# Two-block transformer kernel (RWKV-7, differential attention, gated recurrence) on one core: the down projection of each gated feed-forward moved into its gate/up loop

## The reference, cut to what matters

```python
def swiglu_ffn(h, w_gu, w_down):
    gate, up = jnp.split(h @ w_gu, 2, axis=-1)
    return (jax.nn.silu(gate) * up) @ w_down
# third block: depthwise 3x3 convolution on the gate branch
gc = lax.conv_general_dilated(g2, taps, (1, 1), 'SAME', ..., feature_group_count=f) + conv_b
return (a * jax.nn.gelu(gc, approximate=False)) @ w_down
...
x = x + swiglu_ffn(rms_norm(x, g_ffn[layer]), ffn_w_gu[layer], ffn_w_down[layer])
```

## Time and profile before

| | us |
|---|---|
| median of 3 runs (1563.83 to 1584.23) | 1569.13 |
| profiled execution, span | 1571.6 |
| PE busy in it | 1331.9 (85%) |
| DVE busy | 999.0 (64%) |
| ACT busy | 663.0 (42%) |
| POOL busy | 294.2 (19%) |
| mean granted TensorE clock | 0.913 |

### The profile page before, as it was taken

The page is one execution under the profiler, slowest core; times in us unless marked ns, Lnnn a source line. Parts: engine busy times, 40 slices in busy tenths (PEclk is TensorE's granted clock), DMA queues, the critical chain, the costliest instruction groups (busy, mean ns, idle before and its releaser), DMA issues.

```text
span 1571.6 us, 23032 instructions
## 1 busy us (share of the span) xinstructions
PE 1331.9 (85%) x9712; PEld 1238.5 (79%) x9712; DVE 999.0 (64%) x1265; ACT 663.0 (42%) x844; POOL 294.2 (19%) x229
## 2 busy tenths in 40 slices
PE   3997899997788998989876888999788957887887
PEld 3876889886778997978554778999787947877887
DVE  4859644544489996563755354444549964899953
ACT  3644312114332343456336446543354544544433
POOL 0000332431034551000000001110006502244300
PEclk7978999999888998989987889999898978999999
DMA  7413100000366995544331234545451303444342
GB/s 260 137 67 109 53 1 1 1 1 1 110 238 219 319 323 187 186 135 160 111 104 54 84 118 156 164 163 186 150 182 61 126 8 108 155 141 134 120 148 83
DMA packets 124534, 198.91 MB, mean 127 GB/s; under 512 B 3472, under 2 KB 111376, under 8 KB 118544
## 3 DMA queue, kind: packets, MB, share of 16 engines
q1 hardware_dynamic: 119680, 167.19, 32.5%
q0 software_dynamic: 3456, 25.17, 4.5%
q10 hardware_dynamic: 1296, 5.09, 0.9%
HBM read 196.38 MB, written 1.05 MB: 126 GB/s over the span
## 4 chain that ended last, share of the span: by engine, by line
PE 50%; DVE 26%; issue 10%; ACT 7%; POOL 4%; DMA 2%; DVEq 0%; ACTq 0%; POOLq 0%; SPq 0%
PE bank L564 11%; PE bank L565 11%; PE bank L566 11%; DVE work L1736 6%; DVE ring_r L1479 5%; PE bank L730 3%; PE bank L742 3%; ACT high L1005 2%; PE bank L750 2%; POOL part L1402 2%; POOL ring_r L1409 2%; PE bank L622 1%; DMA buf<-in_wide 1%; DVE buf L1961 1%; DVE buf L1950 1%
## 5 line engine op out<-in xcount | busy, mean ns | idle before, releaser
L564 PE MATMUL bank<-part,high 128*128 128x256 f32 (+1 forms) x2224 | 644.6, 290 | 108.1 <-DVE part L1487 67.9
L565 PE MATMUL bank<-part,high 128*128 128x256 f32 (+1 forms) x2224 | 636.4, 286 | 0.0
L566 PE MATMUL bank<-part,ring_r 128*128 128x256 f32 (+1 forms) x2224 | 635.8, 286 | 0.0
L1479 DVE TENSOR_TENSOR ring_r<-ring,high 128x2048 fp32r<-128x2048 f32 (+2 forms) x172 | 337.4, 1964 | 317.6 <-ACT high L1005 316.9
L564 PEld LDWEIGHTS bank<-part,high 128*128 128x128 f32 (+1 forms) x2224 | 431.5, 194 | 120.1 <-issue 95.4
L565 PEld LDWEIGHTS bank<-part,high 128*128 128x128 f32 (+1 forms) x2224 | 432.3, 194 | 1.1 <-issue 1.0
L566 PEld LDWEIGHTS bank<-part,ring_r 128*128 128x128 f32 (+1 forms) x2224 | 431.1, 194 | 0.1
L1005 ACT ACTIVATE high<-ring 128x2048 fp32r<-128x2048 f32 (+1 forms) x172 | 300.9, 1752 | 171.4 <-PE bank L566 162.5
L1402 POOL TENSOR_TENSOR part<-buf,part 128x256 fp32r<-128x256 f32 x66 | 80.5, 1220 | 536.6 <-ACT part L1059 536.5
L1397 POOL TENSOR_TENSOR work<-buf,con 128x512 f32<-128x512 f32 x56 | 71.1, 1284 | 289.3 <-DVE buf L1660 229.2
L2055 DVE SCALAR_TENSOR_TENSOR buf<-buf,col 128x256 f32<-128x256 f32 x176 | 110.9, 630 | 5.5
(11 more groups left out here) (264 smaller groups left out, 1606.6 us busy)
## 6 DMA issues: line engine op xcount, KB each, us to landing
ring<-in_wide SPq DMA_DIRECT2D x122, 1024.0 KB, 5.7
ring<-in_down SPq DMA_DIRECT2D x48, 704.0 KB, 4.1
buf<-in_wide POOLq DMA_DIRECT2D x24, 1024.0 KB, 5.9
buf<-in_wide ACTq DMA_DIRECT2D x2, 1024.0 KB, 6.5
con<-in_cons SPq DMA_DIRECT2D x1, 1664.0 KB, 11.4
ring<-in_wide SPq DMA_DIRECT2D x2, 576.0 KB, 7.1
buf<-in_ctx_t ACTq DMA_DIRECT2D x1, 1024.0 KB, 4.8
out_t<-resid SPq DMA_DIRECT2D x8, 128.0 KB, 2.1
```

What stands on the lines that cost most here:

```text
L564: mm(bank, ah, bh, start=start, stop=False)
L565: mm(bank, ah, bl, start=False, stop=False)
L566: return mm(bank, al, bh, start=False, stop=stop)
L1479: v.tensor_tensor(low, raw, hi.bitcast(F32), ALU.subtract).then_inc(sem("unit_low"), 1)
```

## The change

The down units are laid out by pair of f instead of by output block: unit c is 128x2048, two f by 1024 output columns, 11 units instead of 16. Unit c-2 follows the two gate/up units of pair c in the stream, and `down_pair(c - 2)` follows `gate_up(c)` on TensorE (`LAG` 2): 48 matmuls that add two f to all eight output blocks, which stay open in banks 0 to 3, two to a bank. Gate/up and side jobs go round over banks 4 to 7. VectorE's multiply frees a gate/up bank instead of GpSimd. The products live in 8 slots, reused once the down unit that read them was used. The last two pairs run after the loop, block by block (96 matmuls). GpSimd's rest of a unit is tied to unit numbers, so that with a down unit in between it looks ahead two f, not three. The splits of the units behind the last down units move behind the next norm's root on ScalarE and behind the applied norm on VectorE (`down_ahead`).

```diff
+PAIR_N = FT // 2
+LAG = 2
+ACTS = 8
+FFN_BANKS = (4, 5, 6, 7)
...
+    def ffn(n):
+        for c in range(PAIR_N):
+            out.extend((f"gu{n}", c, half, "wide", W_AT[f"gu{n}"][0] + c) for half in range(2))
+            if c >= LAG:
+                out.append((f"dn{n}", c - LAG, 0, "down", PAIR_N * n + c - LAG))
+        out.extend((f"dn{n}", c, 0, "down", PAIR_N * n + c) for c in range(PAIR_N - LAG, PAIR_N))
...
     if stage[:2] == "dn":
-        return FT // 2, P
+        return 2, D
...
+        def plan_ffn(n, after_gate=lambda c: (), after_first=()):
+            for c in range(PAIR_N):
+                for i in range(2):
+                    place(("gu", n, 2 * c + i), FFN_BANKS)
+                    unit_job(f"gu{n}", c, i, ("gu", n, 2 * c + i))
+                for key in after_gate(c):
+                    place(key, FFN_BANKS)
+                if c == LAG:
+                    for j in range(KT // 2):
+                        place_at(("dn", n, j), j)
+                if c >= LAG:
+                    unit_mid(f"dn{n}", c - LAG, 0)
+            for key in after_first:
+                place(key, FFN_BANKS)
+            for c in range(PAIR_N - LAG, PAIR_N):
+                unit_job(f"dn{n}", c, 0, ("dn", n, KT // 2 - 1))
...
         def act_value(f):
-            return buf[2 + f // 8][:, f % 8, :]
+            return buf[2][:, f % ACTS, :]
...
+        def wait_act_slot(eng, n, f):
+
+            if f >= ACTS:
+                wait_unit(eng, UNIT_NO[(f"dn{n}", (f - ACTS) // 2, 0)])
...
+                def down_tile(n, f, cb, w):
+
+                    bank = banks[jobs[("dn", n, cb // 2)][0]][:, cb % 2 * S:(cb % 2 + 1) * S]
+                    wl, wh = (z[:, f % 2, cb * P:(cb + 1) * P] for z in w)
+                    mm(bank, wh, act_high(f), start=f == 0 and cb % 2 == 0, stop=False, skip_group_check=True)
+                    mm(bank, wh, act_low(f), start=False, stop=False, skip_group_check=True)
+                    return mm(bank, wl, act_high(f), start=False, stop=f == FT - 1, skip_group_check=True)
+
+                def down_pair(n, c):
+                    w = arrived(f"dn{n}", c, 0)
+                    if c == 0:
+                        for j in range(KT // 2):
+                            open_bank(("dn", n, j))
+                    for f in (2 * c, 2 * c + 1):
+                        pe.wait_ge(sem("act_ready"), FT * n + f + 1)
+                        for cb in range(KT):
+                            last = down_tile(n, f, cb, w)
+                    last.then_inc(sem("unit_used"), 1)
+
+                def feed_forward(n, after_gate=lambda c: None, after_first=lambda: None):
+                    for c in range(PAIR_N):
+                        gate_up(n, c)
+                        after_gate(c)
+                        if c >= LAG:
+                            down_pair(n, c - LAG)
+                    w = [arrived(f"dn{n}", c, 0) for c in range(PAIR_N - LAG, PAIR_N)]
                     for cb in range(KT):
                         if cb == 1:
                             after_first()
...
+                        for f in range(FT - 2 * LAG, FT):
+                            if cb == 0:
+                                pe.wait_ge(sem("act_ready"), FT * n + f + 1)
+                            last = down_tile(n, f, cb, w[f // 2 - PAIR_N + LAG])
+                        if cb % 2:
+                            close(last, ("dn", n, cb // 2))
...
                 def gate_high(n, f):
-                    eng.wait_ge(sem("act_raw"), FT * n + f + 1)
+                    wait_freed(eng, ("gu", n, f))
+                    wait_act_slot(eng, n, f)
...
                         if f % 2:
                             between(f // 2)
+                            if f // 2 >= LAG:
+                                ahead(f"dn{n}", f // 2 - LAG, 0)
 
                 def down(n, norm_no):
 
-                    for cb in range(KT + 2):
...
+                    for j in range(KT // 2):
+                        wait_freed(eng, ("dn", n, j))
+                        square(norm_no, resid, j)
                     root(norm_no)
+                    for c in range(PAIR_N - LAG, PAIR_N):
+                        ahead(f"dn{n}", c, 0)
...
                 def act_low_part(n, f):
...
-                    pool.sem_inc(free[jobs[key][0]], 1)
...
+                def rests_to(stage, u):
+
+                    while rests[0] < FT and UNIT_NO[(stage, rests[0] // 2, rests[0] % 2)] - HIGHS <= u:
+                        low_rest(stage, rests[0])
+                        rests[0] += 1
...
                 for f in range(FT):
-                    if f + HIGHS < FT:
-                        low_rest("gu2", f + HIGHS)
+                    rests_to("gu2", UNIT_NO[("gu2", f // 2, f % 2)])
                     act_low_part(2, f)
...
-                        key = ("dn", n, cb)
-                        for half in range(2):
-                            ahead(f"dn{n}", cb, half)
+                        key = ("dn", n, cb // 2)
                         wait_full(eng, key)
-                        release(add(cb, bank_of(key)[:, 0:S]), key)
...
+                        ins = add(cb, bank_of(key)[:, cb % 2 * S:(cb % 2 + 1) * S])
+                        release(ins, key) if cb % 2 else own.go(ins)
...
-                    v.tensor_tensor(act_value(f), gate_tmp(f), bank_of(key)[:, cols], ALU.mult).then_inc(sem("act_raw"), 1)
+                    wait_act_slot(eng, n, f)
+                    release(v.tensor_tensor(act_value(f), gate_tmp(f), bank_of(key)[:, cols], ALU.mult), key)
...
-                    if f % 2 and f >= 5:
+                    if f % 2 == 0 and f >= 4:
                         modulation_out(f // 2 - 2)
...
                 norm_apply(resid, "hkv", lambda kt: pcol("kv_g", kt))
+                down_ahead(0)
                 norm_apply(resid, "hq", lambda kt: pcol("g_mix1", kt))
...
 def down_chunks(w):
-    w = np.asarray(w).reshape(FT, P, KT, P)
-    return w.transpose(2, 1, 0, 3).reshape(KT, P, FT * P)
+    w = np.asarray(w).reshape(PAIR_N, 2, P, D)
+    return w.transpose(0, 2, 1, 3).reshape(PAIR_N, P, 2 * D)
```

More of the change, by code:

```diff
@@ L74, in wide @@
         out.extend((stage, i, half, "wide", W_AT[name or stage][0] + first + i) for i in range(n) for half in range(2))
-    def down(n):
-        out.extend((f"dn{n}", i, half, "down", KT * n + i) for i in range(KT) for half in range(2))
-    for stage, n in (("k", 2), ("lora1", 1), ("r", 2), ("v", 2), ("o", 2), ("gu0", 11)):
+    def ffn(n):
[4 more added lines that the diff above has]
+        out.extend((f"dn{n}", c, 0, "down", PAIR_N * n + c) for c in range(PAIR_N - LAG, PAIR_N))
+    for stage, n in (("k", 2), ("lora1", 1), ("r", 2), ("v", 2), ("o", 2)):
         wide(stage, n)
-    down(0)
+    ffn(0)
     wide("ak", 2, "kv")
@@ L170, in build, with place_at, place @@
         uses = [0] * NBANK
-        order = []
-        def place(key):
-            b = len(order) % NBANK
+        turn = {}
+        def place_at(key, b):
             jobs[key] = (b, uses[b])
             uses[b] += 1
-            order.append(key)
+        def place(key, among=tuple(range(NBANK))):
+            turn[among] = turn.get(among, -1) + 1
+            place_at(key, among[turn[among] % len(among)])
         unit_end = {}
@@ L257, in build @@
         place(("norm", 1))
[L258 to L262, removed]
+        plan_ffn(0, lambda c: [("ada", c - 1)] if c >= 1 else (), (("ada", 10), ("ada", 11), ("norm", 2)))
         place(("norm", 3))
@@ L289, in build @@
         place(("norm", 4))
[L290 to L299, removed]
+        plan_ffn(1, lambda c: [("csum", d, t) for d in range(2) for t in range(TT)] if c == 4 else
+                 [("cstate", d) for d in range(2)] if c == 7 else ())
         place(("norm", 5))
@@ L328, in build @@
         place(("norm", 6))
-        for c in range(11):
-            plan_gu(2, c)
-        plan_down(2)
+        plan_ffn(2)
         place(("norm", 7))
@@ L635, in down_proj @@
                             after_first()
-                        bank = open_bank(("dn", n, cb))
-                        for half in range(2):
[L638 to L646, removed]
-                                last.then_inc(sem("unit_used"), 1)
+                        for f in range(FT - 2 * LAG, FT):
[4 more added lines that the diff above has]
+                            close(last, ("dn", n, cb // 2))
                 pe.wait_ge(sem("con_in"), 16)
@@ L814, in ada_sum @@
                     close(last, ("ada", c))
-                for c in range(11):
-                    gate_up(0, c)
-                    if c >= 1:
-                        ada_sum(c - 1)
                 def rest_of_context():
@@ L879, in _, with context_states @@
                 norm(4)
-                for c in range(11):
-                    gate_up(1, c)
+                def context_states(c):
                     if c == 4:
@@ L981, in _ @@
                 norm(6)
```

(10 more changed lines are left out.)

72 lines of the change are left out of this document (28 added, 44 removed).

## The result

The changed kernel takes 1621.07 us (median of 4 runs, 1613.41 to 1636.42), the kernel before 1569.1 us: a ratio of 1.0316, 95% interval 1.0232 to 1.0401. It is slower by 3.2%, where 1548 us and no measurable difference were forecast, and it lies outside the range of 1530 to 1569. The profiled execution spans 1614.1 us, 42.5 more than the one of before.

A forecast was written before the change was run, and what follows sets the result against it. Two of three gate/up loops were taken to wait for VectorE, with VectorE half idle in the down projections behind them. Gains of 11, 0 and 10 us, 21 in all, took 1569 to 1548 us; range 1530 to 1569.

The forecast's parts named there:

- the third feed-forward's rounds: Third gate/up loop: rounds of two steps go from 14.8 to 18.7 us, eight of them, putting T(21) 34.1 us later.
- T(f): Third feed-forward: the moment VectorE has done the taps of f; claimed at least T(f-2) plus the loop.
- the loop: Third feed-forward: VectorE's taps through GpSimd, TensorE and ScalarE back to VectorE's split and taps, 19.9 us, becoming the bound.
- the 18.7 to 19.9 of the prediction: Third feed-forward's round: 18.7 us with taps cheaper in VectorE's gaps, 19.9 at the full loop.
- its 14 us over eight rounds: Third feed-forward: by the port-pair rule in full, the sum for eight rounds could be up to 14 us later.
- the down unit in series: Rival: each third-loop round also holds the down unit's 5.64 us, 24.3 us per round, 1593 us in all; chance 0.1.
- TensorE-bound rounds: Rival: third feed-forward's loop shrinks to TensorE's 16.9 us, another 14 us go, 1534 us; chance 0.15.
- first feed-forward: First feed-forward with its boundary: last add 13.6 us earlier, less 2.5 for two splits on ScalarE, 11.1 us earlier.
- second feed-forward: Second feed-forward: -3.7 at the adds, +2.2 for splits, +1.5 bank wait, sum 0, bounds -4 to +4 us.
- the tail: Third feed-forward behind T(21): 15.2 us to the end of TensorE's matmuls instead of 59.6, 44.4 less, plus 0.5 for adds.

The follow-up runs named there:

- experiment 1: Changed kernel, with GpSimd in the third feed-forward taking the rest of unit f+3 before the low part of product f, as before: 1536.22 us, ratio to before 0.9764.
- experiment 2: Kernel before, with GpSimd's rest in the third feed-forward taken two units ahead instead of three: 1711.89 us (one run).
- experiment 3: Changed kernel, with VectorE splitting the whole gate/up unit in the third feed-forward and no rest on GpSimd: 1528.22 us (one run).
- experiment 4: Changed kernel, with ScalarE in the third feed-forward issuing the high part of product f-2 ahead of its wait for unit f: 1582.58 us (one run).
- 5: On experiment 3, ScalarE's two splits behind the norm's root moved behind the following high parts, after the first and second feed-forward: 1525.07 us (one run).
- experiment 6: On experiment 5, the down projection behind the loop takes unit 9 whole, then unit 10 block by block: 1533.74 us, ratio to before 0.9698.
- experiment 7: Kernel before, with VectorE splitting the whole gate/up unit in the third feed-forward and no rest on GpSimd: median 1564.7 us, ratio 0.9919.
- 8: On experiment 6, GpSimd's rest removed in the first feed-forward too, VectorE splitting all 2048 columns: 1520.25 us, ratio to before 0.9642.

## Why the prediction was wrong, and where it was right

**The step that failed** is one sentence of the third feed-forward's rounds: "The change, from f = 6 on, puts the rest of unit f behind product f-3: T(f) is at least T(f-2) plus the loop." The first half holds. The second took the distance from VectorE's T to the unit's start (4.19) from the earlier trace rows and assumed that the high part of product f-3 is issued as soon as VectorE has made the product. In the kernel before the high part did follow closely on T, because ScalarE, in order, had passed its wait for the unit (its grid copy came 4.7 us before T) and stood waiting for VectorE's taps. Its waits over the 100 us of the earlier trace rows:

```profile
ACT buf L1352 <- DVE buf L2055: 31.2, 14, 2.7
```

But `gate_high(f-2)` is the last thing in ScalarE's iteration f, behind `wait_full` of unit f; the high part of product f-3 stands behind unit f-1. The loop was not closed by VectorE's T(f-2) but by TensorE's end of unit f-1: 6.7 us behind the unit before instead of a distance that spans two steps. I had priced a wait and left out what stands in front of the waiting instruction in its own queue. Experiments 1 to 4 show it: the ring appears with the order in either kernel, goes with it, and shrinks to 20.4 us when ScalarE's order is made what I had assumed, near the 18.7 to 19.9 of the prediction but with waits of its own in it.

**What it cost.** T(1) to T(21) took 247.9 us (1338.58 to 1586.49) against 180.2 by the prediction's terms, 67.7 more; the 8 rounds alone are 8 x (27.35 - 18.7) = 69.2. The lower clock behind every second gap, 8.2 - 5.6 = 2.6 us per round, is in that and stood in no term. One reading of the rows was wrong as well, without weight in the sum: of GpSimd's 3.2 us per step only 2.1 lie beside the taps, the first 1.1 beside VectorE's split. By the prediction's own rule the taps could lose at most 2.1 and not 3.2, and its 14 us over eight rounds become 6.

**The rivals.** The named slow case, the down unit in series, gave 1593 us with a similar size and the wrong cause: TensorE's idle times over the 100 us all stand ahead of gate/up units (L569), none ahead of a down unit, and with the down units in place experiment 1 is fast. "TensorE-bound rounds" at 16.9 was set aside because low parts and rests would not fit into the loop; that was right for a loop with the rest behind product f-3. Experiment 1 has TensorE-bound rounds with unchanged durations, by another order.

**Right, first feed-forward** (positions of before, that is 8.1 added to the changed kernel's). Unit 8 starts at 510.3 (511.2 forecast), its wait for the bank of the column sum included; the last gate/up unit is done at 629.8 (629.9); the last add ends at 665.9 (665.2). Rows of the changed kernel that answer to the earlier trace rows:

```profile
502.15 0.35 PE L569 MATMUL bank<-part,high 128*128 128x256 f32 x1 [0.80 <-DVE tiny L1775]
...
621.43 0.28 PE L571 MATMUL bank<-part,ring_r 128*128 128x256 f32 x1
...
655.06 2.73 DVE L1554 TENSOR_TENSOR resid<-resid,bank 128x256 f32<-128x256 f32 x8
...
655.84 2.62 ACT L1038 ACTIVATE buf<-resid 128x512 f32<-128x512 f32 x4 [1.42 <-DVE resid L1554]
```

The gain was 9.2 us, not 11.1: with all eight adds in one row, ScalarE's four squares come behind them in one row too, and the norm is applied 5.5 us behind the last add instead of 4.4. That 1.1 was in no term.

**Right, second feed-forward.** TensorE waited 1.50 us in the context sums, as worked out, and the last add followed TensorE at once; +1.3 us in all against 0 forecast with bounds of -4 to +4. Its parts met less well than the sum: the last add came 1.1 us earlier, where 3.7 - 1.5 = 2.2 were forecast. Rows that answer to the earlier trace rows and, from ScalarE behind the norm's root, to the earlier trace rows:

```profile
979.62 0.70 PE L907 MATMUL bank<-work,con 128*128 128x512 f32 x1 [1.50 <-DVE buf L1561]
...
1109.50 3.69 ACT L1022 ACTIVATE high<-ring 128x2048 fp32r<-128x2048 f32 x2
1113.10 0.61 ACT L1031 ACTIVATE part<-buf 128x512 fp32r<-128x512 f32 x1
```

The first high part stands 8.4 us behind the last add instead of 5.95: 1.8 of the 2.5 are the two splits (2.2 forecast), the other 0.65 is the norm, applied later here too.

**Right, the tail.** From T(21) to the end of the program 27.6 us, 28.0 by the prediction's terms; 44.3 us of the down projection did leave it. The idea of the change, work moved from behind the loop into TensorE's free time, was sound: with experiment 1's order the third feed-forward gains 23 us from the first product to the last add.

**Not settled.** Experiments 2 to 5 have one run each and are read by their stages. How much of experiment 3's lead over experiment 1 in the changed loop is VectorE's cheaper step and how much GpSimd's shorter queue was not separated.

## What to carry to other kernels

A lookahead that is counted in units of one stream changes its meaning when another kind of unit is put into the stream: "three units ahead" had been three steps and became two, on one engine's side job only. For each queue of the loop write down, per iteration, what each instruction waits for and what stands in front of it, and follow a ring through the waits that stand in front, not only through the data; a ring that spans three steps before and two after is the first thing to price. And move a small operation between engines only with its neighbours in view: the rest cost VectorE more as GpSimd's work than as its own, 0.9 us against 0.54 (last section).

## What the runs showed of the hardware

**The first 110 us have more than one length.** TensorE's granted clock from 60 to 110 us was 0.80 in the profiled execution of before, 0.93 in the changed kernel's, 0.66 in experiment 6's and 0.97 in experiment 7's (windows, one fence for each kernel in this order):

```profile
60.00:110.00 50.00, 47.13 (x212) 0.80 0.17 57
```

```profile
60.00:110.00 50.00, 46.35 (x268) 0.93 0.26 89
```

```profile
60.00:110.00 50.00, 45.17 (x146) 0.66 0.15 55
```

```profile
60.00:110.00 50.00, 47.12 (x288) 0.97 0.27 94
```

The first product of the first feed-forward then stood at 449.5, 441.4, 457.0 and 439.2 us, in the order of the clocks, though no edit reaches that stretch. The other six executions fit in: 457.4 at a clock of 0.66 (experiment 2), 452.2 at 0.73 (4), 441.5 to 441.7 at 0.93 (1, 3, 5) and 436.5 at 0.97 (8). What sets the clock there stays open. Of the 8.1 us between the first two, 6.4 are there by the scan on VectorE (106.31 against 99.88 us). Up to 21 us of a run's time are decided before the first feed-forward, more than most edits here are worth. This is why the stages were compared and not the totals.

**GpSimd and VectorE slow each other.** The same low part of 128x256 on GpSimd took 0.74 us while VectorE was idle (experiment 4, at 1442.84) and 2.26 us in the same kernel, beside VectorE's split of 2048 columns:

```profile
1432.22 2.28 DVE L1500 TENSOR_TENSOR ring_r<-ring,high 128x2048 fp32r<-128x2048 f32 x1
...
1432.84 2.26 POOL L1419 TENSOR_TENSOR part<-buf,part 128x256 fp32r<-128x256 f32 x1 [7.15 <-ACT part L1077]
```

The Trainium skill ("SBUF — State Buffer", "Who interferes with whom") says that such instructions block each other on one port pair until the holder is done; by this rule GpSimd is made to wait as well, and its 0.74 against 2.26 us agrees. So does its end: 0.6 us behind the end of the split here, and likewise in the kernel before and in experiment 3 (low part at 1443.30). VectorE loses too: its eight taps took 4.12 us alone, 4.61 in experiments 3 and 7, where only the end of a low part lies beside them, and 5.50 where GpSimd's rest of a unit, 1.45 us, follows it (before). That is 0.9 us for the rest, more than the 0.54 that VectorE needs to do it itself; the difference is the 0.36 of experiment 7's steps.
